# Even step of a fused decoder: decay factor in the exponentials, key weight in the normed key's product, bonus factor on GpSimd, value shift first

## What is computed

```python
xm = p + (prev - p) * mu                       # token shift of r, k, v and the low-rank inputs
w_log = -jax.nn.softplus(-(w0 + jnp.tanh(wl) @ w_up)) - 0.5
decay = jnp.exp(-jnp.exp(w_log))               # = exp(-exp(-0.5) * sigmoid(w0 + ...))
a = jax.nn.sigmoid(a0 + al @ a_up)
kk = heads(k * k_k)
kk = kk / jnp.maximum(jnp.linalg.norm(kk, axis=-1, keepdims=True), 1e-12)
k = k * (1.0 + (a - 1.0) * k_a)

def step(state, inp):                          # over the 256 tokens
    rt, wt, kt, vt, kkt, at = inp
    sa = jnp.einsum('bhvk,bhk->bhv', state, -kkt)
    state = state * wt[:, :, None, :] + sa[..., None] * (kkt * at)[:, :, None, :] + vt[..., None] * kt[:, :, None, :]
    return state, jnp.einsum('bhvk,bhk->bhv', state, rt)

bonus = (jnp.sum(r_h * k_h * r_k, axis=-1, keepdims=True) * v_h)
```

## Time and profile before

| | us |
|---|---|
| median of 3 runs (lowest, highest) | 2582.98 (2582.31, 2583.99) |
| the profiled execution's own time | 2582.0 |
| its span, first to last instruction | 2580.2 |

### The profile page before, as it was taken

One profiled execution on the slowest core, in us unless ns is written; L12 is line 12 of the kernel. 1 busy time (PEld: TensorE's weight loads), 2 busy tenths in 40 slices (PEclk: granted clock), 3 DMA queues, 4 the chain that ended last, 5 costly groups with the idle time before them and its releaser, 6 DMA issues. The chain is left out here.

```text
span 2580.2 us, 53001 instructions
## 1 busy us (share of the span) xinstructions
PE 2533.3 (98%) x19890; PEld 2241.4 (87%) x19890; DVE 1866.7 (72%) x3007; ACT 1273.0 (49%) x1755; POOL 383.0 (15%) x376
## 2 busy tenths in 40 slices
PE   8999999999999999999999999999999999999998
PEld 8988888788888888888888888888888888888887
DVE  6777777676665666666889999998666666666676
ACT  6444444455543444344565656565555334433445
POOL 0111111111110111001111222221111001100112
PEclk9999999999999999999999999999999999999999
DMA  7333333255555555555554454545555555555553
GB/s 264 103 117 117 108 127 109 92 180 179 182 192 187 188 188 186 194 181 195 163 195 165 161 173 157 173 146 196 174 184 195 185 190 181 193 191 183 186 172 131
DMA packets 66019, 437.65 MB, mean 170 GB/s; under 512 B 9456, under 2 KB 10864, under 8 KB 17904
## 3 DMA queue, kind: packets, MB, share of 16 engines
q1 hardware_dynamic: 62064, 435.31, 49.6%
q10 hardware_dynamic: 3840, 0.70, 0.1%
HBM read 433.88 MB, written 2.10 MB: 169 GB/s over the span
## 5 line engine op out<-in xcount | busy, mean ns | idle before, releaser
L314 DVE TENSOR_TENSOR w_low<-w_raw,w_high 128x1024 fp32r<-128x1024 f32 x840 | 1061.6, 1266 | 370.2 <-ACT w_high L309 361.8
L309 ACT ACTIVATE w_high<-w_raw 128x1024 fp32r<-128x1024 f32 x839 | 885.6, 1059 | 867.0 <-PE acc L359 854.5
L324 PE MATMUL acc<-h_split,w_high 128*128 128x512 f32 x3840 | 978.6, 394 | 6.2 <-DVE arena L381 5.1
L324 PEld LDWEIGHTS acc<-h_split,w_high 128*128 128x128 f32 x3840 | 689.2, 189 | 129.5 <-issue 5.4
L359 PEld LDWEIGHTS acc<-h_split,w_low 128*128 128x128 f32 x4576 | 628.5, 191 | 39.9
L359 PE MATMUL acc<-h_split,w_low 128*128 128x256 f32 x4576 | 656.7, 282 | 0.0
L324 PE MATMUL acc<-mix_split,w_high 128*128 128x512 f32 x1904 | 484.9, 394 | 1.6 <-DVE x_residual L926 1.5
L324 PEld LDWEIGHTS acc<-mix_split,w_high 128*128 128x128 f32 x1904 | 340.1, 189 | 62.7 <-DVE x_residual L926 1.7
L487 POOL TENSOR_TENSOR arena<-arena,norm_scale 128x256 f32<-128x256 f32 x152 | 177.3, 1166 | 1418.1 <-DVE arena L381 1418.1
L359 PEld LDWEIGHTS acc<-mix_split,w_low 128*128 128x128 f32 x1904 | 263.1, 190 | 21.7 <-DVE w_low L314 0.6
L359 PE MATMUL acc<-mix_split,w_low 128*128 128x256 f32 x1904 | 269.8, 282 | 0.1
(11 more groups left out here) (277 smaller groups left out, 1540.6 us busy)
## 6 DMA issues: line engine op xcount, KB each, us to landing
w_raw<-w_gu SPq DMA_DIRECT2D x176, 1024.0 KB, 4.8
w_raw<-w_down SPq DMA_DIRECT2D x64, 1024.0 KB, 4.9
w_raw<-w_odd SPq DMA_DIRECT2D x64, 1024.0 KB, 4.9
w_raw<-w_even SPq DMA_DIRECT2D x49, 1024.0 KB, 5.0
w_raw<-w_down SPq DMA_DIRECT2D x32, 768.0 KB, 4.2
w_raw<-w_odd_out SPq DMA_DIRECT2D x12, 1024.0 KB, 5.0
w_raw<-w_even_out SPq DMA_DIRECT2D x10, 1024.0 KB, 4.8
w_raw<-w_even_out SPq DMA_DIRECT2D x6, 896.0 KB, 4.6
```

The lines of the kernel that those rows point to most:

```text
L309: act.activation(wh[:, self.res, ks], raw[:, self.raw, ks], ACT.Copy).then_inc(high_done, 1)
L314: dve.tensor_tensor(wl[:, self.res, ks], raw[:, self.raw, ks], wh[:, self.res, ks].bitcast(F32), ALU.subtract).then_inc(low_done, 1)
L324: pe.matmul(acc[self.acc][:, 0:2 * T], wh[:, self.res, k], flat(both), start=k == 0, stop=stop)
```

## The change

The decay factor -exp(-0.5) leaves the log decay and goes into the scale of ACT's exponentials and into the two middle values. The key times k_k is no longer kept: the product with the reciprocal norm takes key, k_k and norm in one instruction. The bonus factor is made by GpSimd in two products of 128x256, the first after the receptance shift, the second after the key's product (L975). The shifts come in the order key, value, receptance. `rw_prep` counts seven instead of nine, `rw_rk` two instead of one; `rw_kk` is now raised by the normed key's product. Three waits for the shifts move down to the key's product; PE waits for `rw_rk` ahead of the bonus product, and ACT waits for the first of its two counts ahead of the next parameter loads.

```diff
@@ -500,6 +500,12 @@
                 pool.wait_ge(S["at_end"], j + 1)
                 for c in range(2):
                     pool.tensor_tensor(qk[:, c], aqk[:, c], cst[:, C_COS:C_COS + T], ALU.mult).then_inc(S["at_cos"], 1)
+                pool.wait_ge(S["rw_xr"], j + 1)
+                pool.wait_ge(S["rw_par"], 32 * j + 32)
+                pool.tensor_tensor(rkb, xm[:, 0], pj[:, P_RK:P_RK + 1].broadcast_to([P, T]), ALU.mult).then_inc(S["rw_rk"], 1)
+                pool.wait_ge(S["rw_prep"], 7 * j + 3)
+                pool.wait_ge(S["rw_rk"], 2 * j + 1)
+                pool.tensor_tensor(rkb, rkb, d3[:, 0], ALU.mult).then_inc(S["rw_rk"], 1)
                 pool.wait_ge(S["rw_L"], 4 * j + 4)
                 for l in range(1, LEVELS - 2):
 
@@ -622,8 +628,8 @@
                 act.wait_ge(S["rw_b"], 2 * j + 2)
                 act.wait_ge(S["rw_mid"], 2 * j + 2)
                 for c in range(2):
-                    act.activation(e1[:, c], b_sum[:, c], ACT.Exp, bias=nbm[:, c:c + 1]).then_inc(S["rw_e1"], 1)
-                    act.activation(e2[:, c], b_sum[:, c, 1:], ACT.Exp, bias=pbm[:, c:c + 1], scale=-1.0).then_inc(S["rw_e2"], 1)
+                    act.activation(e1[:, c], b_sum[:, c], ACT.Exp, bias=nbm[:, c:c + 1], scale=NEG_EXP_HALF).then_inc(S["rw_e1"], 1)
+                    act.activation(e2[:, c], b_sum[:, c, 1:], ACT.Exp, bias=pbm[:, c:c + 1], scale=-NEG_EXP_HALF).then_inc(S["rw_e2"], 1)
                 act.activation(ebm, pbm[:, 1:2], ACT.Exp).then_inc(S["rw_ebm"], 1)
                 high(4)
 
@@ -636,7 +642,8 @@
                 high(5)
                 if more:
 
-                    waits(act, j + 1, "rw_rk", "rw_t1", "rw_kk", "rw_sq", "rw_a")
+                    waits(act, j + 1, "rw_t1", "rw_kk", "rw_sq", "rw_a")
+                    act.wait_ge(S["rw_rk"], 2 * j + 1)
                     act.dma_start(wa, wa_up[j + 1]).then_inc(S["rw_par"], 16)
                     act.dma_start(pj, par[j + 1]).then_inc(S["rw_par"], 16)
                 act.wait_ge(S["rw_LTR"], 2 * j + 2)
@@ -947,56 +954,52 @@
                 dve.wait_ge(S["rw_par"], 32 * j + 32)
                 dve.tensor_scalar(omka, pj[:, P_KA:P_KA + 1], -1.0, 1.0, ALU.mult, ALU.add).then_inc(S["rw_prep"], 1)
                 dve.tensor_tensor(d3, r3[:, :, 0:T], r3[:, :, 1:], ALU.subtract).then_inc(S["rw_prep"], 1)
-                dve.wait_ge(S["rw_prep"], 9 * j + 2)
-                for c, name in ((1, "rw_xk"), (0, "rw_xr"), (2, "rw_xv")):
+                dve.wait_ge(S["rw_prep"], 7 * j + 2)
+                for c, name in ((1, "rw_xk"), (2, "rw_xv"), (0, "rw_xr")):
                     dve.scalar_tensor_tensor(xm[:, c], d3[:, c], pj[:, P_MU + c:P_MU + c + 1], r3[:, c, 1:],
                                              ALU.mult, ALU.add).then_inc(S[name], 1)
 
                 dve.wait_ge(S["rw_sig"], j + 1)
-                dve.tensor_scalar(lw, lw, NEG_EXP_HALF, None, ALU.mult).then_inc(S["rw_prep"], 1)
-                waits(dve, j + 1, "rw_xk", "rw_xr", "rw_xv")
-                dve.tensor_scalar(d3[:, 1], xm[:, 1], pj[:, P_KK:P_KK + 1], None, ALU.mult).then_inc(S["rw_kk"], 1)
-                dve.wait_ge(S["rw_prep"], 9 * j + 3)
                 for c in range(2):
                     dve.tensor_tensor_scan(b_sum[:, c, 1:], ones, lw[:, c * P:(c + 1) * P], 0.0, ALU.mult, ALU.add).then_inc(S["rw_b"], 1)
                 dve.wait_ge(S["rw_b"], 2 * j + 2)
                 mid = b_sum[:, :, P // 2]
-                dve.tensor_scalar(nbm, mid, -1.0, None, ALU.mult).then_inc(S["rw_mid"], 1)
-                dve.tensor_scalar(pbm, mid, 1.0, None, ALU.mult).then_inc(S["rw_mid"], 1)
+                dve.tensor_scalar(nbm, mid, -NEG_EXP_HALF, None, ALU.mult).then_inc(S["rw_mid"], 1)
+                dve.tensor_scalar(pbm, mid, NEG_EXP_HALF, None, ALU.mult).then_inc(S["rw_mid"], 1)
                 evacuate(-1)
                 low(2)
                 waits(dve, j + 1, "rw_ss", "rw_sq")
                 dve.tensor_scalar(d3[:, 2], bank(2)[:, 0:T], 1e-24, None, ALU.max).then_inc(S["rw_ssmax"], 1)
 
                 dve.wait_ge(S["rw_a"], j + 1)
-                dve.wait_ge(S["rw_prep"], 9 * j + 1)
+                dve.wait_ge(S["rw_prep"], 7 * j + 1)
                 dve.tensor_scalar(d3[:, 0], ag, pj[:, P_KA:P_KA + 1], omka, ALU.mult, ALU.add).then_inc(S["rw_t1"], 1)
                 dve.wait_ge(S["rw_t1"], j + 1)
+                waits(dve, j + 1, "rw_xk", "rw_xr", "rw_xv")
                 dve.tensor_tensor(d3[:, 0], d3[:, 0], xm[:, 1], ALU.mult).then_inc(S["rw_prep"], 1)
-                dve.wait_ge(S["rw_prep"], 9 * j + 4)
+                dve.wait_ge(S["rw_prep"], 7 * j + 3)
                 low(3)
                 dve.wait_ge(S["rw_e2"], 2 * j + 2)
                 dve.tensor_tensor(bk[:, 1], d3[:, 0], flat(e2), ALU.mult).then_inc(S["rw_kt"], 1)
                 dve.wait_ge(S["rw_e1"], 2 * j + 2)
                 dve.tensor_tensor(AR[:, :, 1], xm[:, 0].rearrange("p (c t) -> p c t", c=2), e1[:, :, 1:], ALU.mult).then_inc(S["rw_rt"], 1)
 
-                waits(dve, j + 1, "rw_rn", "rw_kk")
+                waits(dve, j + 1, "rw_rn")
 
                 dve.tensor_tensor(otmp, rn, rn, ALU.mult).then_inc(S["rw_prep"], 1)
-                dve.wait_ge(S["rw_prep"], 9 * j + 5)
+                dve.wait_ge(S["rw_prep"], 7 * j + 4)
                 dve.scalar_tensor_tensor(otmp, otmp, -0.5, d3[:, 2], ALU.mult, ALU.mult).then_inc(S["rw_prep"], 1)
-                dve.wait_ge(S["rw_prep"], 9 * j + 6)
+                dve.wait_ge(S["rw_prep"], 7 * j + 5)
                 dve.scalar_tensor_tensor(otmp, otmp, 1.5, rn, ALU.add, ALU.mult).then_inc(S["rw_prep"], 1)
-                dve.wait_ge(S["rw_prep"], 9 * j + 7)
-                dve.tensor_tensor(d3[:, 1], d3[:, 1], otmp, ALU.mult).then_inc(S["rw_prep"], 1)
-                dve.wait_ge(S["rw_prep"], 9 * j + 8)
+                dve.wait_ge(S["rw_prep"], 7 * j + 6)
+                dve.scalar_tensor_tensor(d3[:, 1], xm[:, 1], pj[:, P_KK:P_KK + 1], otmp, ALU.mult, ALU.mult).then_inc(S["rw_kk"], 1)
+                dve.wait_ge(S["rw_kk"], j + 1)
                 dve.tensor_tensor(AR[:, :, 0], d3[:, 1].rearrange("p (c t) -> p c t", c=2), e1[:, :, 0:P], ALU.mult).then_inc(S["rw_at"], 1)
                 dve.tensor_tensor(d3[:, 2], d3[:, 1], ag, ALU.mult).then_inc(S["rw_prep"], 1)
-                dve.wait_ge(S["rw_prep"], 9 * j + 9)
+                dve.wait_ge(S["rw_prep"], 7 * j + 7)
                 dve.tensor_tensor(bk[:, 0], d3[:, 2], flat(e2), ALU.mult).then_inc(S["rw_bt"], 1)
                 evacuate(0)
                 low(4)
-                dve.scalar_tensor_tensor(rkb, xm[:, 0], pj[:, P_RK:P_RK + 1], d3[:, 0], ALU.mult, ALU.mult).then_inc(S["rw_rk"], 1)
                 dve.wait_ge(S["rw_ebm"], j + 1)
                 dve.tensor_tensor(scl, ebm, e1[:, 0, P:P + 1], ALU.mult).then_inc(S["rw_scl"], 1)
 
@@ -1556,6 +1559,7 @@
                     last = pe.matmul(o, LTR[:, 2 * h + 1, P:2 * P], Us[:, 1, v], start=False, stop=True, skip_group_check=True)
                 last.then_inc(S["rw_y"], 1)
 
+                pe.wait_ge(S["rw_rk"], 2 * j + 2)
                 pe.matmul(bank(0)[:, 0:T], head_ones, rkb, start=True, stop=True).then_inc(S["rw_bonus"], 1)
                 pe.wait_ge(S["rw_late"], 32 * j + 32)
                 pe.matmul(bank(1)[:, 0:T], gu[0:32], sgl[0:32], start=True, stop=True).then_inc(S["rw_g"], 1)
```

## The result

| | kernel before | changed kernel |
|---|---|---|
| median of 20 runs, us | 2583.95 | 2588.64 |
| lowest and highest, us | 2582.31, 2587.75 | 2584.93, 2592.38 |
| the profiled execution's own time, its span, us | 2582.0, 2580.2 | 2588.0, 2586.2 |

The ratio is 1.0019, with a 95% interval of 1.0012 to 1.0025: 4.7 us more. It is slower, clear of the interval, and by the medians within the 0.2% that the prediction called the bound; the upper end of the interval lies beyond it. The changed kernel's lines have new numbers: L1402 is what L1399 was, the first products of bk and AR; L983 was L979, the decayed key; L972 was L969, the sum's floor; L995 was L991; L1000 was L996; L964 the scans; L1433 was L1430. L505 and L508 are GpSimd's two new products.

A forecast was written before the change was run, and what follows sets the result against it. PE bounds the kernel, waiting for DVE's chain at L1399. Eight steps of 0.53 + 0.05 us plus 0.04 in the last make +4.7 us, 2587.6 us against the median 2582.98 (+0.18%, "within 0.2%"); range 2582.8 to 2590.0.

The forecast's parts named there:

- The pin at the sum: DVE at L969 waits 0.30 us for PE's sum of squares, in seven of eight steps; being earlier there gains nothing.
- The second product, +0.53: GpSimd's second product waits out DVE's L314, then delays the decayed key L979 in PE's awaited chain: +0.53 us a step.
- rival (a): GpSimd's second product gets in ahead of DVE's L314, which loses 0.65 us; 2588.6 us in all; chance 0.15.
- L991 as a product of three, +0.05: DVE's product with the reciprocal norm goes from 0.43 to 0.48 us, in the chain: +0.05 us a step.
- The first product, no cost behind the saved 0.49: GpSimd's first product pushes DVE's second scan by about 0.53 us; against 0.49 saved, 0.04 later, inside the 0.30 slack.
- The last step: The one step where DVE has no slack at the sum; the first product's 0.04 us counts there, besides 0.53 and 0.05.
- (b): No overlap: the decayed key L979 starts only when GpSimd's product ends, +0.67 us a step; 2588.8 us; chance 0.07.
- (c): GpSimd's products don't collide with DVE; only L991's 0.05 us a step stays; 2583.4 us; chance 0.14.
- (d): Faster: DVE's saved 0.49 us a step reaches L996, since L969's wait is no pin; 2580.5 or 2579.2 us; chance 0.07.
- (e): GpSimd's first product costs more than the slack at L969, say 0.5 us a step beyond it; 2591.6 us; chance 0.07.

The follow-up runs named there:

- bonus on DVE: The changed kernel with only the bonus factor put back on DVE as one instruction, nothing new on GpSimd; 2583.68 us, ratio 0.9998 to before.
- the late product: The changed kernel, but GpSimd's second product also waits for the last product of bk, so it runs after the chain; 2582.46 us, ratio 0.9996 to before.
- the first four kernels: The four follow-up kernels measured beside the same runs of the kernel before, median 2583.63 us; their own medians are 2583.68, 2587.33, 2582.46 and 2580.60 us.
- the second experiment: The kernel before with only the bonus factor moved to GpSimd, as two products; 2587.33 us, ratio 1.0013 to before.
- two GpSimd products: The changed kernel with GpSimd's second product done twice in a row, the second time on its own result; 2592.97 us, ratio 1.0034 to before.
- The run with the full operand: The changed kernel, GpSimd's first product taking the full cosine table instead of the broadcast bonus weight; one profiled execution, 2593.2 us.
- the key ahead of the sum: The late product, with DVE's two key instructions also moved ahead of the wait for the sum of squares; 2580.60 us, ratio 0.9985 to before.

## Why the prediction was right

- **What bounds the kernel**: PE, by its holes; of the holes, L1399's. It grew by 4.6 us between the two profiled executions, where 4.7 were forecast for the whole.
- **The pin at the sum**: seven waits, and 0.3 us of slack. The bonus on DVE shows it: 0.49 us saved, the wait 0.79 instead of 0.30, and no gain.
- **The second product, +0.53**: L983 took 0.97 for 0.42, +0.55. GpSimd's product took 1.70 (1.1 + 0.58 forecast). It arrived 0.13 behind L314's start (expected 0.05 to 0.15) and did not get in ahead of it: rival (a) didn't occur. Its price, put at 0.65, was seen with the late product, where GpSimd was first by 0.03: 0.57, by 0.08 less. The product's length (0.73 for 0.74) and the 0.13 of L314 hidden under its end were right; the 0.65 had let the product start 0.05 behind the moment at which L314 could, though to go first it must be there before. So which of the two is first hardly matters to DVE here.
- **L991 as a product of three, +0.05**: 0.48 for 0.43 us, and a hole of 0.35 for 0.29 with the bonus on DVE.
- **The first product, no cost behind the saved 0.49**: right for the steps with slack. The second scan was stretched by 0.41, not 0.53, in seven steps, and in step 0 by nothing, since the product is over before the scans. The term was mis-sized: it took the cosine product's 0.58 of holding for a product that is itself 0.12 shorter.
- **The last step**: forecast +0.62, measured 2.10 - 1.78 = 0.32. Of the 0.3 between them 0.16 is the scan there (0.77 against 0.93). The rest is a wait that the forecast had ruled out from step 1 alone, where the reciprocal norm is there 0.24 us before DVE wants it. In the last step of the kernel before, DVE does wait for it:

```profile
473.37 0.42 DVE L981 TENSOR_TENSOR arena<-arena 128x256 f32<-128x256 f32 x1
473.88 0.42 DVE L985 TENSOR_TENSOR arena<-arena 128x256 f32<-128x256 f32 x1
```

```profile
473.34 0.51 ACT L633 ACTIVATE arena<-arena,small 128x256 f32<-128x256 f32 x1
```

L985 starts 0.51 behind L981, in step 1 0.33 (127.34 and 127.67). In the changed kernel the stretched key fills these 0.18 us, and the two instructions stand 0.34 apart (479.72 and 480.06). With the scan's 0.16 that is the 0.30, to some hundredths.

- **Sum**: +4.7 forecast, +4.69 between the medians. The agreement to 0.01 is luck: the interval alone goes from 3.1 to 6.5 us, the misses at the scan and in the last step took away 0.3, the spans of the profiled pair differ by 6.0, and the time itself, forecast as 2587.6, was 2588.64, since the median of before moved from 2582.98 to 2583.95 with more runs. Besides, the first four kernels' runs of before alone reach from 2580.4 to 2586.6 us.
- **Rivals (b) to (e)**: L983 would have been 1.09 by (b), the block in full; it was 0.97. The collision is in all eight steps, against (c). L972 waits in seven steps, against (d) and (e).

The rule of the Trainium skill's page "SBUF — State Buffer", section "Who interferes with whom", held in kind: DVE's instruction with two SBUF inputs and GpSimd's wait for each other's end. The scaling in the second experiment, one SBUF input and stretched from 0.29 to 0.70, agrees with what the same section of the Trainium skill says of `tensor_scalar`, that it can contend in a 2-port mode; no trace here names the mode. In size the trace is 0.14 us below "fully blocks": L983 ends at 130.78, and the product's end at 130.50 plus its own 0.42 would be 130.92.

## What to carry to other kernels

An idle GpSimd is not free for work on data in SBUF: here each product, 0.61 or 0.73 us long, took 0.41 to 0.57 us from a DVE instruction behind its release, so place it beside DVE work for which nobody waits, and find the DVE instruction that it will hold up. Before shortening an engine's chain, find where it waits for the bound engine: what is saved ahead of that wait is worth nothing, and work that can be moved from behind it to ahead of it is worth up to the hole that it closes (here 0.35 us a step for some 0.8 moved). A wait named "issue" in front of the bound engine's instruction can still be a wait for data; the ends of the producers' rows tell.

## What the hardware showed that I had not expected

- With two GpSimd products, L985 and L987 were each stretched by 0.55 us, one product ahead of each, in all eight steps: a waiting product went in behind the one DVE instruction under way, though DVE had the next ready. That isn't so every time. In step 1 of the same kernel the first product arrived during the first scan, as in other steps, and got in only behind the second, which kept its 0.40 us; it then held up a scaling of 128x2 (0.40 us where it is 0.17 in step 1 of the changed kernel). The run with the full operand shows the same in its step 1.

```profile
123.61 0.73 DVE L966 TENSOR_TENSOR_SCAN arena<-constants_sb,arena 128x128 f32<-128x128 f32 x2
124.38 0.40 DVE L969 TENSOR_SCALAR small<-arena 128x2 f32<-128x2 f32 x1
```

```profile
123.87 0.88 POOL L505 TENSOR_TENSOR arena<-arena 128x256 f32<-128x256 f32 x1 [3.26 <-DVE arena L961]
```

- Nor does the order of the starts decide alone, where they are this close. With the key ahead of the sum, the late product starts 0.02 us before the weight split in step 1 and in step 2. In step 2 the split takes 1.78 us and the product 0.73; in step 1 the split keeps its 1.22 and the product takes 1.83.
- For the same shape on GpSimd, the first product held up a scan or a scaling by 0.41 us, and the second a product or a weight split by 0.55 to 0.57. The first is 0.12 us shorter by itself; the operand's form explains 0.02 of that.
- The runs of the changed kernel spread over 7.5 us, those of before over 5.4, in 20 runs each; the granted clock of the changed kernel's runs went from 0.998 in the fastest (2584.93) to 0.995 in the slowest (2592.38). The spread goes with the clock: 0.003 of 2588 us is 7.8.
